# Two key gathers of the next quarter in front of the value gathers of a quarter, in the expert stage of a decoder layer

## The reference

```
u = jnp.take(u_tab, ec, axis=0)
act = jax.nn.gelu(jnp.einsum('cd,ced->ce', hc, u), approximate=False)
wgt = gc * act
vr = jnp.take(v_tab, ec, axis=0)
return jnp.einsum('ce,ced->cd', wgt, vr)
```

## Time and profile before

| what | us |
|---|---|
| median of 3 runs | 1971.66 (1970.85 to 1972.91) |
| the profiled execution, its own time | 1972.74 |
| its span, first to last instruction | 1970.4 |
| PE busy in it | 1358.7 (69%) |
| DVE busy | 1257.7 (64%) |
| POOL busy | 1098.4 (56%) |
| ACT busy | 597.6 (30%) |
| key gathers, issue to landing, median | 8.2 |
| value gathers, issue to landing, median | 7.5 |

### The profile page before, as it was taken

The page is one execution under the profiler, slowest core; times in us unless marked ns, Lnnn a source line. Parts: engine busy times, 40 slices in busy tenths (PEclk is TensorE's granted clock), DMA queues, the critical chain, the costliest instruction groups (busy, mean ns, idle before and its releaser), DMA issues.

```text
span 1970.4 us, 23769 instructions
## 1 busy us (share of the span) xinstructions
PE 1358.7 (69%) x7318; PEld 864.6 (44%) x7318; DVE 1257.7 (64%) x3101; ACT 597.6 (30%) x1657; POOL 1098.4 (56%) x1062
## 2 busy tenths in 40 slices
PE   6998999857888678989877876444443444544444
PEld 5887799845655444667555553111110111111111
DVE  3265436477777888867778856666667666666640
ACT  2446424233344255322223432112212112211110
POOL 0100010166666477766855767777777776677764
PEclk8999999979989889888898897656566655666567
DMA  9755245599999899999999999999999999999997
GB/s 362 258 186 212 97 156 201 196 374 409 409 408 384 329 373 360 403 410 385 409 405 392 406 409 403 409 404 403 407 408 402 404 403 404 367 409 407 402 396 288
DMA packets 202447, 701.87 MB, mean 356 GB/s; under 512 B 22569, under 2 KB 32369, under 8 KB 202033
## 3 DMA queue, kind: packets, MB, share of 16 engines
q0 software_dynamic: 149760, 545.33, 70.1%
q1 hardware_dynamic: 52560, 155.02, 21.6%
HBM read 691.26 MB, written 11.06 MB: 356 GB/s over the span
## 4 chain that ended last, share of the span: by engine, by line
DMA 20%; issue 13%; PE 12%; POOL 11%; DVE 9%; ACT 2%; POOLq 0%; DVEq 0%; SPq 0%; ACTq 0%
DMA arena<-in_v_tab,pku 13%; POOL arena L2196 11%; PE y L1171 6%; DMA arena<-in_u_tab,pku 6%; DVE arena L2021 4%; PE acc L806 4%; DMA arena<-in_xT 1%; ACT arena L1264 1%; DVE pku L2042 1%; PE acc L946 1%; DVE arena L1753 0%; PE turned L1151 0%; DVE pk L2041 0%; DVE pk L2057 0%; DVE pku L2058 0%
## 5 line engine op out<-in xcount | busy, mean ns | idle before, releaser
L2196 POOL DMA_INDIRECT arena<-in_u_tab,pku x520 | 550.9, 1060 | 356.9 <-issue 150.5
L1171 PE MATMUL y<-arena 128*32 128x512 f32 x2080 | 411.5, 907 | 467.2 <-DMA arena<-in_v_tab,pku 467.2
L2196 POOL DMA_INDIRECT arena<-in_v_tab,pku x520 | 532.4, 1024 | 255.5 <-issue 148.2
L806 PE MATMUL acc<-arena 128*128 128x264 f32 (+1 forms) x2304 | 556.4, 400 | 18.6 <-ACT arena L1308 8.1
L806 PEld LDWEIGHTS acc<-arena 128*128 128x128 f32 x2304 | 451.0, 199 | 128.2 <-issue 53.5
L2021 DVE CUSTOM_DVE_ANT_0 arena<-arena,h_bank 128x1024 f32<-128x1024 f32 x240 | 291.0, 1219 | 252.3 <-DMA arena<-in_u_tab,pku 251.8
L1171 PEld LDWEIGHTS y<-arena 128*32 128x32 f32 x2080 | 82.7, 143 | 710.7 <-issue 703.4
L2021 DVE CUSTOM_DVE_ANT_0 arena<-arena 128x1024 f32<-128x1024 f32 x280 | 335.1, 1222 | 83.4 <-DMA arena<-in_u_tab,pku 68.4
L1507 ACT ACTIVATE pk<-pk 128x1 f32<-128x1 f32 x520 | 103.6, 281 | 2.1
L1529 ACT CAST pku<-turned 128x8 uint32<-128x8 f32 x64 | 10.4, 162 | 283.8 <-PE turned L1151 256.9
L2239 POOL TENSOR_TENSOR o_lo<-arena,o_hi 128x256 fp32r<-128x256 f32 x8 | 6.6, 863 | 156.8 <-ACT o_hi L1383 156.8
(11 more groups left out here) (249 smaller groups left out, 1822.7 us busy)
## 6 DMA issues: line engine op xcount, KB each, us to landing
arena<-w_mod SPq DMA_DIRECT2D x48, 512.0 KB, 5.5
arena<-w_pq SPq DMA_DIRECT2D x32, 512.0 KB, 6.9
arena<-w_xr SPq DMA_DIRECT2D x20, 512.0 KB, 8.2
arena<-w_qk SPq DMA_DIRECT2D x20, 512.0 KB, 7.7
arena<-w_gr SPq DMA_DIRECT2D x20, 512.0 KB, 6.9
arena<-w_rnn SPq DMA_DIRECT2D x16, 640.0 KB, 6.6
arena<-in_u_tab,pku POOLq DMA_INDIRECT x520, 8.2
arena<-in_v_tab,pku POOLq DMA_INDIRECT x520, 7.5
```

What stands on the lines that cost most here:

```text
L806: mm = pe.matmul(a[:, 0:n], w[:, k, :], rhs[:, k, 0:n], start=(k == 0), stop=(k == ks - 1))
L1171: mm = pe.matmul(y[rows, h, :], spread[g % NTURN][:, 32 * j:32 * j + 32], rows_v[j][:, h * 512:(h + 1) * 512], start=first and (g != SAMPL ...
L2196: pool.indirect_dma_start(out=row, out_offset=None, in_=table, in_offset=bass.IndirectOffsetOnAxis(ap=idx, axis=0), **more).then_inc(signa ...
```

## The change

The constant `U_AHEAD` = 1 is added. GpSimd's quarter 0 now issues key gathers 0 to 3, and quarter k issues 2k+2 and 2k+3, up to the last; the value gathers of a quarter stay. All other lists stay.

```
-DOTS_LAG, NAMES_LEAD, TURN_LEAD, SUMS_LAG = 2, 6, 2, 2
+U_AHEAD, DOTS_LAG, NAMES_LEAD, TURN_LEAD, SUMS_LAG = 1, 2, 6, 2, 2
...
             for k in range(len(V_AT)):
-                us = [2 * k, 2 * k + 1] if k < U_QUARTERS else []
+                us = [n for n in range(2 * (k + U_AHEAD) if k else 0, 2 * (k + U_AHEAD) + 2) if n < U_SLOTS]
                 vs = list(V_AT[k])
                 while us or vs:
                     if us:
```

## The result

The changed kernel takes 1990.73 us (median of 7 runs, 1985.39 to 1997.59) where the kernel before, beside it, takes 1971.27 us: a ratio of 1.0087 [1.0071, 1.0103], or +17.2 us [14.0, 20.3]. The forecast was 1976.4 us with a range up to 1985, so the sign was right and the size was not. The profiled execution took 1990.73 us.

The account below looks back on a forecast made before the run. The prediction held that bytes set the time, so only dips could be won or lost. Its terms, 1.7 - 2.6 + 1.3 + 1.7 + 0 + 2.6 = +4.7 us, on a median of 1971.66 made 1976.4 us, range 1965 to 1985.

Parts of the forecast that it names:

- (a): Start to the first value gather: the list is the same, 23 key gathers, so 0.
- (b): 430 to 620 us: two keys more in front land a value row 3.4 us later; ends 0 and +3.4, taken +1.7.
- (c): 620 to 800 us: two more keys issued when GpSimd stands at a value gather; ends -2.6 and 0, taken -2.6.
- key places not free: Upper end, 0 us, of the 620 to 800 us term: the keys cannot be issued early.
- (d): 840 to 940 us: GpSimd stands at key gathers with one value less issued; ends 0 and +1.3, taken +1.3.
- (e): 940 to 1060 us: a value row 3.4 us later delays sums, norm, dot products; ends 0 and +3.4, taken +1.7.
- (f): 1220 to 1900 us: values land two gathers later, but two more lie in front; ends -2.6 and +2.6, taken 0.
- (g): The end: a value row two gathers later delays the last names; ends -3.0 and +2.6, taken +2.6.
- keys are what the dips lack: Rival, faster: earlier keys help in the dips and the last wait for names goes; 1966.1 us, chance 0.22.
- the lead cancels: Rival: sooner key rows and later value rows offset each other everywhere; time 1971.7 us, chance 0.33.

Follow-up runs that it names:

- the run with only the fourth row late: Kernel before, up to quarter 128 the value rows of each four moved behind 0, 0, 0, 2 more keys: 1986.18 us, 1.0063.
- the fourth row keeps its place: Kernel before, up to quarter 128 the value rows of each four moved behind 2, 2, 1, 0 more keys: 1977.35 us, 1.0028.
- the eight places: Kernel before with eight key places in place of nine (UPLACES = 8), its list kept: 1978.21 us, 1.0032.

## Why the prediction was wrong, step by step

(a) The start, 0: right.

(b) 430 to 620 us, +1.7 in the forecast, is one of the two steps that failed; +7.1 us [4.5, 9.5] by the run with the lead in quarters 0 to 39, 9.8 us between dot 20 and dot 70 of the two traces. The chain was the right one (value row, sums, dense work), and the run with only the fourth row late bears it out. Two choices in the size were wrong. First, "two keys more in front put a value row 2 x 1.70 = 3.4 us later" takes a key in front as one gather. That holds while GpSimd issues without a stand (v0 to v3); here it came to stand at keys, 31.9 us after 9.3 us in this stretch, and then, as I read it, a key is one dot product, 3.38 us (v12 to v15: 5.3 to 7.1 us for two). The text had said that "if it waits, the values behind it in the list now wait too" and put no price on it. Second, I took the middle between 0 and 3.4, since keys come sooner. VectorE's earlier keys give nothing back (its waits fell from 12.4 to 8.3 us in this stretch, and the dot products came later all the same), and more than one set of sums pays: the waits at sums 0, 2 and 10 each grew by 3 to 4 us (2.2 to 6.1, 5.5 to 8.4, 6.7 to 9.6), while three smaller ones went (at sums 1, 4 and 6). At sums 0 to 12 together TensorE's idle time grew from 26.4 to 32.8 us, near the loss.

(c) 620 to 800 us, -2.6; measured -0.6 us [-3.7, +2.6] by the run with the lead in quarters 40 to 68, +0.2 us between dots 70 and 150. The sign that I had named, a higher rate from 640 to 700 us, came out, 327 and then 370 GB/s, but it does not show the mechanism:

```profile
640.00:700.00 60.00, 43.41 (x210) 28.96 (x209) 52.24 (x131) 19.21 (x57) 31.32 (x29) 0.91 0.87 327
```

```profile
640.00:700.00 60.00, 46.13 (x213) 30.38 (x212) 49.22 (x123) 22.26 (x58) 33.35 (x33) 0.91 0.97 370
```

The dip of before now begins earlier: from 560 to 640 us the rate fell from 393 to 350 GB/s, and over 560 to 700 us it is 365 before and 358 after. The run with the lead in quarters 0 to 39 has 359 GB/s from 640 to 700 us, with no lead in that stretch. The run with the lead in quarters 40 to 68 is the fair one: 349 GB/s there, 371 from 620 to 840 us (before 365), and no gain in time. So the step from bytes to time is not borne out, though -2.6 us is inside that run's interval. My reading is that the rows moved early are keys; they lie in their places until the dense work lets their dot products go, and GpSimd then stands at the next keys (34.2 us for key places from 620 to 800 us in the changed kernel, 9.3 in before). By that my upper end, "key places not free", was the case.

(d) and (e) 840 to 1060 us, +3.0 together, is the other step that failed; +9.1 us [5.3, 12.8] by the run with the lead in quarters 40 to 128 (with (c) in it), 7.3 us between dot 150 and dot 220 of the two traces. The 3.4 us between sums 42 and 44 come behind it; for 1060 to 1220 us the forecast had no term and gave no reason. The same mis-sized term as in (b): in (d) I had GpSimd standing at keys seven times and priced one value row less at 1.28 us, where by my reading the value behind it comes one or two dot products later. TensorE's waits from 840 to 1060 us do not show it (24.7 us before, 24.4 after), as the later kernel has other work in that window; its idle time at sums 29 to 43 does, 27.6 and then 40.4 us. (d) also said that TensorE and not the data time that stretch; the four around 937 us, for which it did not wait in before, show how near the data were. The chain of the earlier trace rows is the same one after, 14 us later (sums at 1060.82 for 1046.38, the norm at 1078.28 for 1064.01), and the standing key of the earlier trace rows stands as long as before:

```profile
1060.82 3.64 PE y L1171 x16
...
1078.28 1.81 DVE arena L1640
```

```profile
1088.12 1.15 POOL L2196 DMA_INDIRECT arena<-in_u_tab,pku  x1 [7.82 <-issue]
```

I had looked for a norm 2 to 6 us later.

(f) 1220 to 1900 us, 0: in the two traces right to 0.5 us (sums 50 at +18.1, sums 120 at +18.0). In a kernel that comes to this stage without a delay, the lead costs 5 us all the same, no more than the end of +2.6 and the +2.6 of (g) together; so the runs do not bear out the 0 taken here.

(g) The end, +2.6: the last wait for names grew as foretold in sign, from 3.32 to 4.90 us and not to 5.9, and the last sums lost 0.5 us more than sums 120.

```profile
1933.75 0.17 ACT L1529 CAST pku<-turned 128x8 uint32<-128x8 f32 x1 [17.72 <-PE turned L1151]
```

```profile
1934.26 0.94 POOL L2196 DMA_INDIRECT arena<-in_v_tab,pku  x1 [4.90 <-ACT pku L1529]
```

Of the rivals, "keys are what the dips lack" did not come: more bytes in the dip gained no time, and TensorE's waits grew. And "the lead cancels" holds in (f) of the whole change alone. The rule of the Trainium skill ("DMA: Bandwidth & Descriptors", section "Queues, rings and completion order") that queues take turns would have put the sum 1.7 us higher, at 6.4; no run here separates it from the rest.

Open: the 5 us that are left when the fourth row keeps its place, the 5 us of the last stage, and the loss of the eight places behind 930 us. A list with more than nine key places, which would take away the stands without touching the order, was not tried. The price of a key as one dot product, too, is read from the traces and not tested by itself.

## What to carry to other kernels

A list that one engine works off in order has two rates: that of its own work while it never stands, and that of whatever frees its places when it does. Before you price "two more in front", look in the waits which of the two the list has in that stretch. If it stands, the duration of the thing that frees a place (here a dot product between dense work, 2.7 to 3.4 us) is nearer than that of a transfer (1.28 us). Where a consumer takes rows in groups, look at the last of a group first: here it brought 12.4 of some 16 us, and the other three 5.5. And compare waits over the same work, not only over the same window.

## What the runs showed that I had not expected

A higher transfer rate in a dip is not a gain by itself: with the lead in quarters 40 to 68 alone, 349 GB/s from 640 to 700 us after 327 left the time where it was. And 22 us more of GpSimd's stands at keys between 430 and 840 us (19.4 to 41.4 us, eight places; 14.6 us less at values) moved nothing behind them up to dot 130. A stand can be covered while rows are queued. Row v7 of the changed kernel was issued at 450.42 us and landed 9.5 us later, at 459.90, with rows queued in front of it; key 32, issued at 459.85 us when all earlier gathers were about to land, landed after 5.2 us. So by estimate about 4 us of the first was queue, and a stand much longer than that (8.48 us at key 32) is seen by the transfers: from 460 to 466 us they run at 226 GB/s, in before at 407.
